# An encoder block with two kinds of attention: the second score product of the GQA heads in two row groups, with the query rows copied to the upper partitions

## What is computed

```python
q_g = _rope_2d(_rmsnorm(q_g...), pos_row, pos_col)      # 8 heads x 64
k_g = _rope_2d(_rmsnorm(k_g...), pos_row, pos_col)      # 2 heads x 64
...
s = jnp.einsum('bqgrd,bkgd->bgrqk', qb, k_g) * scale_g
p = jax.nn.softmax(s, axis=-1)
o = jnp.einsum('bgrqk,bkgd->bqgrd', p, v_g)
```

## Time and profile before

| | |
|---|---|
| median of three runs | 2997.29 us (2993.71 to 2999.22) |
| the profiled execution | 2994.37 us, span 2992.6 us |
| mean granted TensorE clock | 0.972 |
| TensorE matmuls busy | 2826.5 us, 94% of the span |
| VectorE, ScalarE, POOL busy | 61%, 49%, 23% |
| score matmuls (L1388), both kinds of head | 1392, 379.0 us busy |
| chain that ended last | TensorE 21% of the span, nothing else over 1% |

### The profile page before, as it was taken

The page is one execution under the profiler, slowest core; times in us unless marked ns, Lnnn a source line. Parts: engine busy times, 40 slices in busy tenths (PEclk is TensorE's granted clock), DMA queues, the critical chain, the costliest instruction groups (busy, mean ns, idle before and its releaser), DMA issues. The chain is left out here.

```text
span 2992.6 us, 56058 instructions
## 1 busy us (share of the span) xinstructions
PE 2826.5 (94%) x20084; PEld 2619.8 (88%) x20084; DVE 1820.7 (61%) x3158; ACT 1479.4 (49%) x2701; POOL 684.4 (23%) x1247
## 2 busy tenths in 40 slices
PE   8999899999999999999999999999965999999994
PEld 7888698999998888887999999988844999999994
DVE  6777767888887777676334334433345555555555
ACT  4333336888887777677223223321222445544443
POOL 0000013444443333334000000000013233332331
PEclk9999898999999999999999999999976999999997
DMA  6556592202113224443757564456655898889977
GB/s 212 158 157 191 152 377 86 71 24 72 50 33 93 75 74 108 102 125 99 225 137 228 160 203 132 144 174 197 190 138 141 198 207 199 201 203 209 207 161 260
DMA packets 529044, 461.87 MB, mean 154 GB/s; under 512 B 53458, under 2 KB 464802, under 8 KB 528880
## 3 DMA queue, kind: packets, MB, share of 16 engines
q1 hardware_dynamic: 510256, 411.74, 48.0%
q0 software_dynamic: 16256, 47.89, 7.5%
q10 hardware_dynamic: 2368, 0.16, 0.0%
HBM read 315.57 MB, written 144.14 MB: 154 GB/s over the span
## 5 line engine op out<-in xcount | busy, mean ns | idle before, releaser
L1576 DVE TENSOR_REDUCE t_peak<-t_s_ps 128x1 f32<-128x1024 f32 (+2 forms) x276 | 336.8, 1221 | 84.8 <-PE t_s_ps L1388 83.9
L1388 PE MATMUL t_s_ps<-t_k,t_q 96*128 96x512 f32 (+2 forms) x1392 | 379.0, 402 | 4.8 <-ACT t_probs L1492 4.8
L1840 PE MATMUL c_acc<-c_tokens,c_w_hi 128*128 128x260 f32 x2048 | 373.0, 283 | 4.5 <-DVE c_w_lo L1913 4.5
L1601 DVE TENSOR_TENSOR t_pt_lo<-t_tp,t_pt_hi 128x512 fp32r<-128x512 f32 x552 | 336.4, 650 | 36.1 <-ACT t_pt_hi L1522 35.5
L1522 ACT CAST t_pt_hi<-t_tp 128x512 fp32r<-128x512 f32 x552 | 284.7, 565 | 113.0 <-PE t_tp L1418 112.0
L1840 PEld LDWEIGHTS c_acc<-c_tokens,c_w_hi 128*128 128x128 f32 x2048 | 316.8, 189 | 4.8 <-issue 4.8
L1492 ACT ACTIVATE t_probs<-t_s_ps,t_bias 128x1024 f32<-128x1024 f32 (+2 forms) x276 | 308.2, 1117 | 22.8 <-POOL t_bias L1655 8.1
L2445 PE MATMUL e_gu<-e_x_hi,w_hi 128*128 128x260 f32 x1024 | 293.7, 287 | 0.9 <-DVE e_x_lo L2650 0.9
L2445 PE MATMUL e_gu<-e_x_lo,w_hi 128*128 128x260 f32 x1024 | 289.9, 283 | 0.0
L1840 PE MATMUL c_acc<-c_tokens,c_w_lo 128*128 128x260 f32 x1024 | 289.8, 283 | 0.0
L2445 PE MATMUL e_gu<-e_x_hi,w_lo 128*128 128x260 f32 x1024 | 289.6, 283 | 0.0
(11 more groups left out here) (299 smaller groups left out, 6569.2 us busy)
## 6 DMA issues: line engine op xcount, KB each, us to landing
c_raw<-in_w_in SPq DMA_DIRECT2D x64, 512.0 KB, 5.6
w_raw<-in_w_gate SPq DMA_DIRECT2D x64, 512.0 KB, 6.9
w_raw<-in_w_up SPq DMA_DIRECT2D x64, 512.0 KB, 9.3
w_raw<-in_w_down SPq DMA_DIRECT2D x64, 512.0 KB, 4.5
c_tokens<-o_t SPq DMA_DIRECT2D x32, 520.0 KB, 6.7
c_tokens<-hn_t SPq DMA_DIRECT2D x16, 1040.0 KB, 9.3
r_mt<-mix_t SPq DMA_DIRECT2D x32, 512.0 KB, 5.2
mix_t<-c_out_hi SPq DMA_DIRECT2D x32, 260.0 KB, 2.1
```

What stands on the lines that cost most here:

```text
L1388: ins = pe.matmul(s_ps[0:r, n % 2, half * 512:(half + 1) * 512], query(n, a), key(n, c, half * 512, (half + 1) * 512), start=(at == 0), st ...
L1576: dve.tensor_reduce(peak[0:r, b % 2, i:i + 1], s_ps[0:r, n % 2, :], AX_X, ALU.max).then_inc(peak_done, 1)
L1601: dve.tensor_tensor(pt_lo[span], tp[:, f % RING, :].rearrange("p (t n) -> p t n", t=4)[:, :, 0:r], pt_hi[span].bitcast(F32), ALU.subtract) ...
L1840: pe.matmul(acc[:, b, mixer, 0:W], w[:, parity, mixer, k, :], tokens[t % 2][:, part, k, cols], start=(k == 0 and at == 0), stop=(k == DK - ...
```

## The change

The second product (key part 1, the low part) is no longer done over 128 partitions. It becomes two matmuls over 64 partitions each, both with the high part of the queries only: keys 0 to 511 with partitions 0 to 63 of `q` and `k`, keys 512 to 1023 with partitions 64 to 127 of `k` and of a new tile `raised`, which holds a copy of the queries' high rows on the upper partitions. The term query low x key low is left out by this. The sums go to the same two banks as before. MLA is as it was, and so are GQA's meta scores.

The new tile has four buffers of one block's 3 x 128 queries. SP fills them by a transfer from SBUF to SBUF, 64 partitions x up to 384 words, one a GQA block (44 in all), two blocks ahead: in turn b, between `load_qk` and `store(b - 1)`; before turn 0's load for blocks 0 and 1. It waits for the unit's queries, and for the scores of the block that used the buffer before. TensorE waits for the transfer at the first chunk of each GQA block, ahead of its first 64-row matmul.

```diff
+    RAISED = 4
...
+        raised = sb("raised", [P, RAISED, WIDE], F32R)
...
+            def raise_queries(b):
+
+                if b >= BLOCKS or units[unit_of(b)][0]:
+                    return
+                u = unit_of(b)
+                at = chunks[b * PER][1]
+                sp.wait_ge(qk_loaded[u % 2], qk_after[u])
+                if b >= RAISED:
+                    sp.wait_ge(s_filled, (b - RAISED + 1) * PER)
+                sp.dma_start(raised[HD:P, b % RAISED, 0:width(b)].bitcast(F32), q[u % 2][0:HD, at:at + width(b)].bitcast(F32))\
+                    .then_inc(raised_loaded[b % RAISED], 16)
+
             last_unit = first_block[len(units) - 1]
             for b in range(BLOCKS):
                 u = unit_of(b)
                 starts = first_block[u] == b and u + 1 < len(units)
+                if b == 0:
+                    raise_queries(0)
+                    raise_queries(1)
                 if starts:
                     load_qk(u + 1)
+                raise_queries(b + 2)
                 if b > 0:
                     store(b - 1)
                 if starts:
@@
-            def passes(n):
-                return [(0, 0), (0, 1), (1, 0)] if units[chunks[n][0]][0] else [(0, 0), (0, 1)]
+            def by_halves(n):
+
+                (u, at, r), b, i = chunks[n], n // PER, n % PER
+                if i == 0:
+                    pe.wait_ge(raised_loaded[b % RAISED], 16 * (b // RAISED + 1))
+                pe.matmul(s_ps[0:r, n % 2, 0:512], q[u % 2][0:HD, at:at + r], k[0:HD, u % 2, 1, 0:512], start=False, stop=True)
+                return pe.matmul(s_ps[0:r, n % 2, 512:SEQ], raised[HD:P, b % RAISED, i * P:i * P + r],
+                                 k[HD:P, u % 2, 1, 512:SEQ], start=False, stop=True)
@@
-                todo = passes(n)
+                mla, p = units[chunks[n][0]][0], chunks[n][0] % 2
+                todo = [(0, 0), (0, 1), (1, 0)] if mla else [(0, 0)]
                 for at, (a, c) in enumerate(todo):
                     for half in range(2):
                         ins = pe.matmul(s_ps[0:r, n % 2, half * 512:(half + 1) * 512], query(n, a),
                                         key(n, c, half * 512, (half + 1) * 512),
-                                        start=(at == 0), stop=(at == len(todo) - 1))
+                                        start=(at == 0), stop=(bool(mla) and at == 2))
+                if not mla:
+                    ins = by_halves(n)
                 ins.then_inc(s_filled, 1)
```

More of the change, by code:

```diff
@@ L1240, in attention @@
         qk_loaded, v_loaded = held.qk_loaded, held.v_loaded
+        raised_loaded = [sem(f"raised_loaded{k}") for k in range(RAISED)]
         stored = [sem("stored0"), sem("stored1")]
```

## The result

The changed kernel took 3084.51 us (median of four runs, 3083.57 to 3087.85) against 2996.65 us for the kernel before (four runs): a ratio of 1.0296, 95% interval 1.0278 to 1.0313. It is slower by 88 us; 103 were forecast, in a range of 43 to 143. The profiled execution has a span of 3082.6 us, 90.0 over that of before, and all but half a microsecond of it arises in the GQA units: from the start of the meta scores of block 1 to that of the first MLA block's, the trace of before counts 400.5 us, that of after 490.0.

A forecast was written before the change was run, and what follows sets the result against it. TensorE was taken to bound the GQA stage. Product 28, two-piece blocks 8, long copy stops 49 and clock 18 sum to 103 us: 2994.4 + 103 = 3097 us (3100 on the median), range 3040 to 3140.

The forecast's parts named there:

- What bounds the stage: GQA stage: each TensorE microsecond is one of the span; ScalarE would end last only if a chunk shrank over 0.35 us.
- The switch: Each GQA chunk: going from full rows to 64-row products and back costs 0.33 us a round trip.
- What the overlap gives back: Each GQA chunk: second half starts 0.11 us after the first, giving back 0.12; net +0.21 x 132 = +28 us.
- Rival 2: GQA 64-row products start side by side: 14 us less than forecast, 3086 us; chance 0.16.
- Rival 1: GQA 64-row halves don't overlap at all: 16 us more than forecast, 3116 us; chance 0.2.
- The copies, (a) to (d): Query-row copies on SP's queue: ordinary blocks 0, blocks behind two-piece stores +8 us, (c) and (d) together +49 us.
- (c): Blocks 13, 24, 35: copy stands behind the next unit's load, late by 10.3, 10.1 and 9.5 us before 0.5 slack each.
- (d): Blocks 14, 25, 36: copy stands behind a unit's ten last stores, late by 7.1, 7.8, 7.1 us before 0.5 slack.
- The blocks with two pieces: Eight blocks whose copy stands behind a store in two pieces: 1 us late each, +8 us.
- Rival 3: Copies held up only by issue time, not queue bytes: 3078 us, or 3025 if not late at all; chance 0.15.
- The clock: Half clock on TensorE after six long stops of 7 to 10 us: 6 x 3 = +18 us.
- Rival 4: GQA products: second half streams beside the first, row groups change without a drain, 30 us gained; chance 0.05.

The follow-up runs named there:

- the run in the same rows: Changed kernel without copies or their wait, both halves of the second product on the lower 64 partitions; 3043.35 us, ratio 1.0165.

## Why the prediction was right, point by point

- **What bounds the stage.** Right for a change that adds to TensorE: what was added came out in the span. The other side was taken too wide: ScalarE was to take over only when a chunk shrank by over 0.35 us, and the run without the second half got 24.6 of 30 us at 0.23.
- **The switch.** Forecast from the 64-query chunks of before at 0.33 us a round trip, measured 0.36 by the run in the same rows. Nothing in its two holds was new: the idle of 0.37 us before the load is the same number as in the earlier trace rows.
- **What the overlap gives back.** This step was wrong in size. I took a start one weight load apart and 0.12 given back, since loads came one behind another in every row of before; the loads of different row groups start together too, and all of the 0.23 came back. Rival 2 had it (+0.10 forecast, +0.13 measured): 17 us (132 x 0.13) in place of 28. The Trainium skill's rule, products in distinct row groups starting about 4 ns apart ("TensorE: Matmul & The Clock Gate", Part 3), agrees with this trace, in which both start at 634.25. Rival 1 (no overlap) is excluded.
- **The copies, (a) to (d).** Right in place, and in size in the sum: 49 us of long stops forecast, 48.6 measured. That it fits to within a microsecond is luck: (c) was 2 us too high and (d) 2 us too low. By places 10.3, 10.1 and 9.5 less 0.5 each for (c) against 8.67, 8.63 and 8.99; 7.1, 7.8 and 7.1 less 0.5 for (d) against 7.48, 7.80 and 7.04. For block 13 the order was right, the copy landed just behind the small rest of the load; but the rest took 9.4 us here and not the 10.6 of before. The blocks with two pieces gave 9.2 us, forecast 8, and three ordinary ones, put at nothing, 2.4. Rival 3 falls: 96 KB behind 2 MB took 9.0 us and not 2.2. That most ordinary copies stay just in time only because the product is slower was forecast (0.2 late against 0.5 of slack), and the run with full products shows the other side of it, 0.24 a block.
- **The clock.** 18 us forecast at 3 a stop, 12.8 measured, 2.1 a stop. The term was sized from 6.0 us of work at half speed behind a stop in MLA; here the half clock lasted 4.5 us beyond the restart in the mean, of which half is lost.
- **Sum.** 28 + 8 + 49 + 18 = 103 against 17.2 + 11.6 + 48.6 + 12.8 = 90.2, each term read from the trace and not from what the others leave; the spans say 90.0. Two terms were too high, by 11 and 5 us, and one too low, by 4.
- **Rival 4** needed a switch without a hold. It has one in every chunk.

## What to carry to other kernels

Two products of 64 rows side by side save one stream, here 0.23 us, but going into the half-row use of the array and out again costs more, here 0.36 us; by these numbers it would take at least two such pairs between one pair of switches before it can pay, an estimate that no run here tried. A helper transfer that TensorE waits for must be timed against the worst place of its queue, behind the largest load and the longest run of stores, and not against its own latency: asked for two blocks ahead they cost 71 us, four blocks ahead, with the same buffers and bytes, nothing. And a price measured in one variant isn't the price in another: a slower product hid 19 us of late copies.

## What the runs showed of the hardware

Weight loads of different row groups start together (both at 634.25), unlike all loads of full rows, which came one behind another; the pair costs what one product costs. Eight transposes of 64 rows, in pairs, took 0.24 us up to the next group, and the two passes of a chunk together 0.60 (0.24 and 641.62 - 641.26), where eight full ones take 0.87. Stops of about 1 us (521.94, 0.95 us of wait) left the product behind them at 0.49 us, full clock; each stop of 7 us or more was followed by half clock. Between them lie two that went different ways: in the run with the copy ahead of the load a stop of 1.75 us was followed by some 3.4 us of half clock, while one of 1.85 us in the changed kernel was not. The half clock around the start of attention, from 455 us on, is from one run to another 12 to 30 us long (13 before, 30 in the run in the same rows), and moves the first blocks by up to 4 us; why it differs wasn't explained.
